# Preparing latent attention inside the last projection blocks, passing GLA and pool results through DRAM, and starting the projection in half blocks

## The chip, the cores and the metric

One core of a Trainium2 chip runs the whole kernel. The metric is the device time of one execution in microseconds, the median of several. The engines named below are TensorE (PE, with its weight loads as PEld), VectorE (DVE), ScalarE (ACT), GpSimd (POOL) and SyncE (SP), which issues most of the DMAs.

## The reference, cut to what matters

Two sequences (1024 and 512 tokens, so 1536 in all, width 1024) pass one encoder layer:

```python
h = rmsnorm(x, norm_g)
z = einsum('bsd,de->bse', h, w_in)          # c_q 256, c_kv 128, k_rope 64, gate_mla 512, u_pool 256, gate_pool 256,
                                            # q_gla, k_gla 128 each, v_gla 256, lr_fwd, lr_bwd 16 each, gate_gla 256
q  = rmsnorm(c_q) @ w_uq                    # 4 heads of 128 + 64 rotary
kv = rmsnorm(c_kv) @ w_ukv                  # 4 heads of 128 key + 128 value
p  = softmax((q_nope k_nope^T + rope(q_rope) rope(k_rope)^T) * MLA_SCALE)
o_mla = p v
o_pool = pool_mixer(u_pool)                 # centred means over windows 2, 4, 8, 16
o_gla = gla_mixer(...)                      # gated linear attention, forward and backward
mixed = concat(o_mla * silu(gate_mla), o_pool * silu(gate_pool), o_gla * silu(gate_gla))
y = rmsnorm(x + mixed @ w_out, final_norm_g)
```

## The kernel before

Features lie on the 128 partitions and tokens along the row, in three column blocks of 512 tokens (`BLK`, `TB = 3`). Every float32 product is made of three products of split operands (`product`, L75 to L79): each operand is a rounded `hi` and a remainder `lo`, and hi x hi, hi x lo and lo x hi are added in PSUM. ScalarE makes the `hi` parts; VectorE or GpSimd makes the `lo` parts by subtraction.

There are four phases, one after the other. Each ends only when all five engines have ended it, SP's waits on its DMAs among them.

- `phase_front` normalises x tile by tile (12 tiles of 128 tokens), turns the tiles with transposes into `h_hi` and `h_lo`, and multiplies by the input weights: 18 weight tiles (`ORDER`) times 3 column blocks are 54 blocks of 24 products (`project`). The first 6 blocks (`EARLY_BLOCKS`) are interleaved with the turns. Weight tile `o` is loaded by `load_w`, its hi part made by ScalarE in `split_hi`, its lo part by GpSimd in `split_lo`; one raw slot serves all tiles from the third on. Between the halves of the blocks stands the work of the gated linear attention (GLA) and the pooling (`mixing`, `compare`, `output`, `spread`), which ends around block 43. Tiles 7 to 14 of the order are the gates: `empty` copies them to `z_gate` and ScalarE's queue stores them to `gates_scratch`. The last three tiles are the latents `c_kv` and `c_q`, which stay in SBUF as rows of `z`, as do the results of the GLA; those of the pooling go to `pool_scratch` and come back.
- `phase_mla_prepare` normalises the latents, builds the query weights `w_q` (`w_uq` times `w_uk`), turns the tokens, makes the rotary queries (`rope_queries`, three column groups of 12 products) and rotates them on VectorE (L1317, L1322, L1289). SP stores them to `rope_scratch` in twelve DMAs (L1201) and then copies `mla_k_rope` onto the lower 64 partitions (L1204).
- `phase_mla_attend` makes scores, softmax and values for 4 heads.
- `phase_output` gates the mixed rows (GpSimd, `weight_gates`), splits them and multiplies by `w_out`, in a loop over pairs of token tiles, then adds x, normalises and stores.

The order of work on each engine is the order in which the code is written. Only semaphores join the engines, so a wait holds up all that follows in the same queue.

Of the kernel before, what the change touches and what calls it, by code (L numbers as in the profile page):

```python
# [44 lines left out]
def rows_of(t):  # L45
    return bass.ds(t * P, P)
# [28 lines left out]
def product(nc, out, a_hi, a_lo, b_hi, b_lo, first=True, last=True):  # L75
# [17 lines left out]
ORDER = (Z_LR, Z_U, Z_U + 1, Z_K, Z_V, Z_V + 1, Z_Q) + tuple(range(Z_FIRST_GATE, Z_FIRST_GATE + Z_GATES)) + \  # L93
    (Z_CKV + Z_GATES, Z_CQ + Z_GATES, Z_CQ + Z_GATES + 1)
FIRST_GATE_AT = 7
# [9 lines left out]

SPLITS = (32, 16, 8, 4, 2, 1)
# [16 lines left out]

def gla_point(i, half):

    return 2 * (i - FIRST_LEVEL_BLOCK) + half - 1


def phase_front(nc, cx, dram, gates_dram, pool_dram, k_rope_dram, h_hi, h_lo, z, psum, ident, sums):
# [5 lines left out]
    with ExitStack() as mem:  # L135
# [8 lines left out]
        sb("z_state_pad", [P, P // 4])  # L144
        gate_up = sb("z_gate_up", [P, 2, P])
# [42 lines left out]

        q, k = z[:, Z_Q, :], z[:, Z_K, :]
        values = z[:, Z_V:Z_V + 2, :]  # L190
# [5 lines left out]
        half_set = sem("n_half_set")  # L196
        squares_done = sem("n_squares_done")
# [25 lines left out]
        pool_back = sem("g_pool_back")  # L223
# [70 lines left out]
        def _(sp):  # L294
# [9 lines left out]

            load_x(0)
# [27 lines left out]
            sp.wait_ge(attn_mm, TILES)  # L333
            sp.dma_start(z[:, Z_U:Z_U + 2, :], pool_dram.rearrange("a p t -> p a t")).then_inc(pool_back, 16)
            sp.wait_ge(pool_back, 16)
# [4 lines left out]
        def _(act):  # L340
# [20 lines left out]
            def empty(i):  # L361
# [4 lines left out]
                if FIRST_GATE_AT <= o < FIRST_GATE_AT + Z_GATES:  # L366
                    if i >= TB * FIRST_GATE_AT + 2:
                        act.wait_ge(gate_stored[i % 2], 16 * ((i - TB * FIRST_GATE_AT) // 2))
                    nc.scalar.activation(stage[:, i % 2, :], bank, ACT.Copy).then_inc(z_emptied, 1)  # L369
                    if i > TB * FIRST_GATE_AT:  # L370
                        store_gate(i - 1)
                elif tile == Z_Q:
                    nc.scalar.activation(z[:, Z_Q, t], bank, ACT.Copy, scale=2.0 * GLA_Q_SCALE).then_inc(z_emptied, 1)
                else:
                    if tile == Z_V and tb == 0:
                        act.wait_ge(pool_step, POOL_STEPS)
                    if i == TB * (FIRST_GATE_AT + Z_GATES):
                        store_gate(i - 1)
                        act.wait_ge(o_mm, TILES)
# [1666 lines left out]
```

## Time and profile before

| | us |
|---|---|
| median of 3 runs | 852.72 |
| lowest to highest | 852.43 to 853.53 |
| the profiled execution | 853.92 |
| its span, first to last instruction | 852.1 |
| TensorE busy in the span | 767.0 (90%) |
| VectorE, ScalarE, GpSimd busy | 417.1, 333.3, 195.8 |
| mean granted TensorE clock | 0.966 |

All times in the rows are counted from the start of the span. Busy shares are means over phases with different limits, so they are read phase by phase: the front ends at 400.56 (TensorE's last product), the preparation at 457.96, attention at 695.58. TensorE has two clock levels, 2.4 and 1.2 GHz; the granted clock of a stretch is its mean share of the higher one. In the records from 0 to 30 us it reads 1.00 although the products stand 0.42 us apart, as they do elsewhere at 0.50; there the spacing is the better sign.

### The profile page before, as it was taken

The page shows a single profiled execution, that of the slowest core. Times are in us where ns is not written, and L with a number is a line of the kernel's source. Part 1 is how long each engine was busy: PE and PEld are TensorE (multiplying, and loading weights), DVE is VectorE, ACT ScalarE, POOL GpSimd, SP SyncE. Part 2 cuts the span into 40 slices and gives each one's busy share as a digit, 9 for nine tenths or more (in the row PEclk, how much of TensorE's full clock was granted, in tenths as well). Part 3 has the DMA queues.
Part 4 walks back from the last instruction along what each step waited for, and adds up shares of the span by engine and source line. Part 5 has one row for each costly group of instructions (what it writes and reads, how often), then busy time and mean ns, then how long its engine had stood idle before and what let it go on. Part 6 is the DMA issues. An engine that isn't in the chain of part 4 may idle for free. (4 is left out here: it accounts for less than half of the span.)

```text
span 852.1 us, 14303 instructions
## 1 busy us (share of the span) xinstructions
PE 767.0 (90%) x5936; PEld 637.4 (75%) x5936; DVE 417.1 (49%) x699; ACT 333.3 (39%) x570; POOL 195.8 (23%) x223
## 2 busy tenths in 40 slices
PE   3899999999999999998845899999999947999996
PEld 2786778788888878887744688888888845788885
DVE  5734766475565310000771566666667746433332
ACT  6441545334545323111530544444444553233321
POOL 2312125464454212110340000000000026233320
PEclk9999999999999999999676999999999987999999
DMA  7402021011111111400533000000033020444431
GB/s 274 126 12 63 26 95 41 27 40 64 64 50 40 54 65 60 148 23 22 167 100 88 12 13 14 13 20 18 13 106 131 1 98 27 147 149 148 148 123 49
DMA packets 32443, 61.37 MB, mean 72 GB/s; under 512 B 3296, under 2 KB 16000, under 8 KB 32384
## 3 DMA queue, kind: packets, MB, share of 16 engines
q1 hardware_dynamic: 26384, 46.36, 16.9%
q10 hardware_dynamic: 6000, 14.16, 4.3%
q8 instruction: 44, 0.72, 0.4%
q14 instruction: 15, 0.12, 0.0%
HBM read 42.42 MB, written 17.69 MB: 71 GB/s over the span
## 5 line engine op out<-in xcount | busy, mean ns | idle before, releaser
L77 PE MATMUL psum<-h_hi,z_w_hi 128*128 128x512 f32 x432 | 174.4, 404 | 3.8 <-DVE h_lo L697 3.8
L79 PE MATMUL psum<-h_hi,z_w_lo 128*128 128x512 f32 x432 | 169.0, 391 | 0.0
L78 PE MATMUL psum<-h_lo,z_w_hi 128*128 128x512 f32 x432 | 168.8, 391 | 0.0
L77 PEld LDWEIGHTS psum<-h_hi,z_w_hi 128*128 128x128 f32 x432 | 81.5, 189 | 24.3 <-DVE h_lo L697 4.6
L79 PEld LDWEIGHTS psum<-h_hi,z_w_lo 128*128 128x128 f32 x432 | 81.4, 189 | 17.6
L78 PEld LDWEIGHTS psum<-h_lo,z_w_hi 128*128 128x128 f32 x432 | 81.6, 189 | 16.4 <-issue 0.7
L1544 ACT ACTIVATE a_weights<-psum,a_bias,mla_q_scale 128x1024 f32<-128x1024 f32 (+1 forms) x48 | 51.1, 1064 | 103.8 <-DVE a_bias L1583 103.8
L77 PE MATMUL psum<-o_w_hi,o_m_hi 128*128 128x512 f32 x192 | 76.7, 400 | 15.4 <-DVE o_w_lo L1871 14.4
L78 PE MATMUL psum<-o_w_lo,o_m_hi 128*128 128x512 f32 x192 | 75.8, 395 | 0.0
L79 PE MATMUL psum<-o_w_hi,o_m_lo 128*128 128x512 f32 x192 | 75.7, 394 | 0.0
L1607 DVE TENSOR_TENSOR a_turned_lo<-psum,a_turned_hi 128x512 fp32r<-128x512 f32 x80 | 52.3, 687 | 41.7 <-ACT a_turned_hi L1561 41.7
L1752 POOL TENSOR_TENSOR mla_mixed<-mla_mixed,o_gate_first 128x512 f32 (+1 forms) x6 | 7.7, 1283 | 278.8 <-ACT o_gate_first L1787 278.8
L589 POOL TENSOR_TENSOR z_w_lo<-z_w_raw,z_w_hi 128x1024 fp32r<-128x1024 f32 x17 | 42.7, 2514 | 89.3 <-ACT z_w_hi L359 89.3
L828 DVE COPY_PREDICATED g_attn<-g_level_mask,psum 128x256 f32<-128x256 int32 x72 | 32.5, 451 | 59.0 <-ACT g_attn L476 56.9
L77 PEld LDWEIGHTS psum<-o_w_hi,o_m_hi 128*128 128x128 f32 x192 | 36.8, 192 | 24.9 <-issue 12.4
L1580 DVE TENSOR_REDUCE a_top<-psum 128x1 f32<-128x1024 f32 (+1 forms) x48 | 49.9, 1039 | 9.3 <-PE psum L1637 9.3
L381 ACT ACTIVATE z<-psum 128x512 f32<-128x512 f32 x27 | 15.9, 599 | 87.8 <-PE psum L79 87.8
L369 ACT ACTIVATE z_gate<-psum 128x512 f32<-128x512 f32 x24 | 14.3, 598 | 90.9 <-PE psum L79 90.9
L1645 PE MATMUL psum<-ident,a_weights 128*128 128x128 f32 x320 | 44.5, 276 | 5.5 <-DVE a_turned_lo L1607 5.5
L1645 PEld LDWEIGHTS psum<-ident,a_weights 128*128 128x128 f32 x320 | 35.7, 140 | 13.3 <-issue 8.9
L77 PE MATMUL psum<-a_turned_hi,mla_tokens_hi 128*128 128x256 f32 x160 | 44.8, 280 | 0.3 <-DVE a_turned_lo L1607 0.3
L79 PE MATMUL psum<-a_turned_hi,mla_tokens_lo 128*128 128x256 f32 x160 | 44.7, 279 | 0.0
(212 smaller groups left out, 1493.2 us busy)
## 6 DMA issues: line engine op xcount, KB each, us to landing
z_w_raw<-in_w_z_dram SPq DMA_DIRECT2D x17, 512.0 KB, 3.4
n_x_in<-in_x_dram SPq DMA_DIRECT2D x12, 512.0 KB, 4.1
gates_scratch<-z_gate ACTq DMA_DIRECT2D x24, 256.0 KB, 2.0
o_x_in<-in_x_dram SPq DMA_DIRECT2D x12, 512.0 KB, 3.5
out_dram<-o_y ACTq DMA_DIRECT2D x12, 512.0 KB, 2.6
o_w_raw<-in_w_out_dram SPq DMA_DIRECT2D x8, 512.0 KB, 9.6
a_q_rope<-rope_scratch SPq DMA_DIRECT2D x12, 256.0 KB, 2.6
o_gate_first<-gates_scratch SPq DMA_DIRECT2D x6, 512.0 KB, 5.3
```

The source lines that it names most:

```text
L77: nc.tensor.matmul(out, a_hi, b_hi, start=first, stop=False)
L78: nc.tensor.matmul(out, a_hi, b_lo, start=False, stop=False)
L79: return nc.tensor.matmul(out, a_lo, b_hi, start=False, stop=last)
L369: nc.scalar.activation(stage[:, i % 2, :], bank, ACT.Copy).then_inc(z_emptied, 1)
L381: nc.scalar.activation(z[:, place, t], bank, ACT.Copy).then_inc(z_emptied, 1)
L589: nc.gpsimd.tensor_tensor(w_lo[:, o % 2, :], raw_of(o)[:, :], w_hi[:, o % 2, :].bitcast(F32), ALU.subtract).then_inc(w_lo_ready, 1)
L828: nc.vector.copy_predicated(attn[:, t % 2, :, :], level_mask[:, n, :].bitcast(mybir.dt.int32).unsqueeze(1).broadcast_to([P, HEADS, CHUNK]) ...
L1544: nc.scalar.activation(weights[:, m % SLOTS, 0:count * P].rearrange("p (a k) -> p a k", k=BLK), psum[:, banks, :], ACT.Exp, bias=bias[:, m ...
L1580: nc.vector.tensor_reduce(top[:, m:m + 1], psum[:, banks, :], mybir.AxisListType.XY, ALU.max)\
L1607: nc.vector.tensor_tensor(turned_lo[at], psum[:, 4 + item % 2, :].rearrange("p (k q) -> p k q", k=4), turned_hi[at].bitcast(F32), ALU.subt ...
L1645: mm = nc.tensor.transpose(psum[:, 4 + item % 2, k * P:(k + 1) * P], weights[:, m % SLOTS, (4 * n + k) * P:(4 * n + k + 1) * P], ident[:, :])
L1752: nc.gpsimd.tensor_tensor(mla_mixed[:, :, rows_of(n)], mla_mixed[:, :, rows_of(n)], gate[s][:, 0:4, :], ALU.mult).then_inc(gated, 1)
```

## The change

1. `phase_mla_prepare` is gone; its steps stand inside `phase_front`. The latents move up in `ORDER`, ahead of the last two gate tiles: tile 13 is `c_kv`, 14 and 15 are `c_q`, 16 and 17 are gates. `prepare_attention` puts the steps between the half blocks of blocks 40 to 52. The latents are read from PSUM twice (a copy or scaled copy, and a Square for the sums of squares), and the lo part of `c_q` is made from PSUM.
2. The GLA and pool results are stored to `mix_scratch` and loaded per token tile in the output phase (`load_mix`).
3. The six early blocks are made in halves of 256 columns (`project_early`), the first after two tiles of x. The first two weights are loaded and split earlier.
4. TensorE first makes 14 products of zeros, and 5 after each of the first two turns (`keep_running`).
5. Tiles in SBUF are placed anew. `sum_latent_squares` sums four columns of 128 tokens a block, on a PSUM bank of its own.

TensorE, first instructions of the front. Before (L885 turns a tile of x, L77 to L79 are the products):

```order
L885 MATMUL psum<-ident,n_x_norm 128x128 x32
L77 MATMUL psum<-h_hi,z_w_hi 128x512
L78 MATMUL psum<-h_lo,z_w_hi 128x512
L79 MATMUL psum<-h_hi,z_w_lo 128x512
L77 MATMUL psum<-h_hi,z_w_hi 128x512
```

The same place now (L1479 are the products of zeros, L1195 turns a tile):

```order
L1479 MATMUL psum<-z_idle 128x512 x14
L1195 MATMUL psum<-ident,n_x_norm 128x128 x8
L1479 MATMUL psum<-z_idle 128x512 x5
L1195 MATMUL psum<-ident,n_x_norm 128x128 x8
L1479 MATMUL psum<-z_idle 128x512 x5
L1195 MATMUL psum<-ident,n_x_norm 128x128 x8
L77 MATMUL psum<-h_hi,z_w_hi 128x256
L78 MATMUL psum<-h_lo,z_w_hi 128x256
L79 MATMUL psum<-h_hi,z_w_lo 128x256
```

The first product now follows three turns, not four, and has half the columns.

SP, the end of the front and the preparation before (`rope_scratch` takes the turned queries; four such stores stand for each of three groups, the last group is shown):

```order
L1201 DMA rope_scratch<-p_rope0hi 4x32x512 [waits p_rope_hi]
L1201 DMA rope_scratch<-p_rope1hi 4x32x512 [waits p_rope_hi]
L1201 DMA rope_scratch<-p_rope0lo 4x32x512 [waits p_rope_lo]
L1201 DMA rope_scratch<-p_rope1lo 4x32x512 [waits p_rope_lo]
L1204 DMA mla_k_rope<-mla_k_rope 64x1536 [waits p_k_rope_hi]
L1117 UNCONDITIONAL_BRANCH [waits p_k_stacked,p_rope_stored]
```

SP at the end of the front now, from the load of the last weight tile on (the first of three groups is shown, then the end of the phase, after eight more stores):

```order
L386 DMA z_w_raw<-in_w_z_dram 128x1024 [waits z_w_lo_ready]
L446 DMA p_w_rope<-in_w_rope_dram 128x512 [waits z_w_lo_ready]
L448 DMA mla_k_rope<-mla_k_rope 64x1536 [waits p_k_rope_hi]
L453 DMA rope_scratch<-p_rope_split_147 4x32x512 [waits p_rope_hi]
L453 DMA rope_scratch<-p_rope_split_149 4x32x512 [waits p_rope_hi]
L453 DMA rope_scratch<-p_rope_split_146 4x32x512 [waits p_rope_lo]
L453 DMA rope_scratch<-p_rope_split_148 4x32x512 [waits p_rope_lo]
...
L152 UNCONDITIONAL_BRANCH [waits z_gate_stored0,p_rope_stored,z_gate_stored1,p_k_stacked,g_mix_stored]
```

The copy of `mla_k_rope` has moved ahead of the stores; their shape is unchanged, and the phase still ends with a wait for them.

The diff, cut to its core:

```diff
+ROPE_AT = {(51, 0): 0, (52, 0): 1, (52, 1): 2}
 # SP, front
+            load_w(0)
             load_x(2)
+            load_w(1)
             load_x(3)
-            load_w(0)
-            load_w(1)
...
+                if o == 12:
+                    store_mix(0)
...
+            sp.wait_ge(w_lo_ready, Z_TILES)
+            sp.dma_start(w_rope[:, :, :, :], dram["w_rope"]).then_inc(w_rope_loaded, 16)
+            sp.wait_ge(k_rope_hi, 1)
+            sp.dma_start(keep.k_rope[ROPE:P, :].bitcast(F32), keep.k_rope[0:ROPE, :].bitcast(F32)).then_inc(k_stacked, 16)
+            for tb in range(TB):
+                t = slice(tb * BLK, (tb + 1) * BLK)
+                for n, (part, ready) in enumerate(((1, rope_hi), (3, rope_hi), (0, rope_lo), (2, rope_lo))):
+                    sp.wait_ge(ready, 2 * tb + n % 2 + 1)
+                    sp.dma_start(rope_dram[:, n * HALF_ROPE:(n + 1) * HALF_ROPE, t],
+                                 rope_split[tb][part][:, :].bitcast(F32)).then_inc(rope_stored, 16)
+            sp.wait_ge(rope_stored, 64 * TB)
 # ScalarE, front
-                if n in (1, 2):
-                    split_hi(n - 1)
+                if n < 2:
+                    split_hi(n)
+                if i == 40:
+                    take_w_v()
+                if i == 41:
+                    take_w_q()
+                if i == 43:
+                    take_kv_mean()
+                if i == 44:
+                    fill_kv_rows()
+                if i == 46:
+                    take_ckv()
+                if i == 48:
+                    take_k_rope()
+                if i == 49:
+                    take_q_mean()
+                    take_tokens()
+                if i == 50:
+                    take_w_rope()
+                if i >= 51:
+                    take_rope(i - 51)
 # GpSimd, front
-                if n in (4, 5):
-                    split_lo(n - 4)
+                if n in (2, 3):
+                    split_lo(n - 2)
...
+            split_lo(17)
+            pool.wait_ge(k_rope_hi, 1)
+            subtract(keep.k_rope_lo[0:ROPE, :], k_swapped[:, :], keep.k_rope[0:ROPE, :]).then_inc(k_rope_lo, 1)
+            invert_means(rstd, q_mean_ready, q_root_step)
...
+            subtract(w_rope_lo[:, :, :, :], w_rope[:, :, :, :], w_rope_hi[:, :, :, :]).then_inc(w_rope_lo_ready, 1)
 # VectorE, front, after the GLA
+            split_tokens()
+            rotate(0)
+            split_rope(0)
+            rotate(1)
+            rotate(2)
+            split_rope(1)
+            split_rope(2)
 # TensorE, front
+            def prepare_attention(i, half):
+                if (i, half) == (W_Q_BLOCK, 0):
+                    make_w_q()
+                if half and SQUARES_AT < i <= SQUARES_AT + SQUARES:
+                    sum_latent_squares(i - 1 - SQUARES_AT)
+                if (i, half) == (KV_ROWS_BLOCK, 0):
+                    pe.wait_ge(kv_rows_ready, 1)
+                    pe.wait_ge(mixed, TB)
+                    turn_to_bank(kv_rows).then_inc(kv_rows_mm, 1)
+                if (i, half) == (TOKENS_BLOCK, 1):
+                    pe.wait_ge(ckv_ready, 1)
+                    turn_to_bank(ckv).then_inc(tokens_mm, 1)
+                if (i, half) in ROPE_AT:
+                    rope_queries(ROPE_AT[i, half])
+            def project_early(j):
+                o, tb, part = j % 2, j // 4, j // 2 % 2
+                pe.wait_ge(w_lo_ready, o + 1)
+                pe.wait_ge(lo_ready, 8 * tb + 4 * part + 4)
...
+            keep_running(14)
+            for n in range(3):
                 turn(n)
+                if n < 2:
+                    keep_running(5)
+            for j in range(2 * EARLY):
+                project_early(j)
+                if j + 3 < TILES:
+                    turn(j + 3)
 # output phase, SP and GpSimd
+                    sp.wait_ge(m_lo_ready, 2 * (2 * i + s) - 2)
+                    load_mix(i, s)
-                nc.gpsimd.tensor_tensor(z[:, Z_V:Z_V + 4, rows_of(n)], z[:, Z_V:Z_V + 4, rows_of(n)], gate[s][:, 4:8, :],
-                                        ALU.mult).then_inc(gated, 1)
+                pool.wait_ge(mix_loaded[s], 16 * i + 16)
+                nc.gpsimd.tensor_tensor(mix[s][:, :, :], mix[s][:, :, :], gate[s][:, 4:8, :], ALU.mult).then_inc(gated, 1)
```

`W_Q_BLOCK`, `KV_ROWS_BLOCK` and `TOKENS_BLOCK` are 41, 45 and 46; `SQUARES_AT` is block 39 and `SQUARES` 9.

## Rows read from the trace of the kernel before

**Rows 1.** Busy time by stretch: start:end, length, engines, clock, DMA share, GB/s.

```profile
67.03:400.56 333.53, 328.84 (x3569) 267.19 (x3568) 139.10 (x256) 122.58 (x211) 110.22 (x124) 1.00 0.15 54
400.56:457.96 57.40, 28.71 (x161) 26.45 (x161) 33.56 (x34) 19.55 (x21) 17.17 (x11) 0.68 0.43 126
```

**Rows 2.** Waits of TensorE from 400 us on: total us, times, longest.

```profile
PE psum L77 <- PEq L1117: 22.2, 1, 22.2
...
PE psum L77 <- DVE o_m_lo L1847: 1.0, 1, 1.0
```

**Rows 3.** SP's queue in order of time: start us, us, instruction.

```profile
419.82 0.66 SPq L1201 DMA_DIRECT2D rope_scratch<-p_rope0hi  x1
...
442.14 2.33 SPq L1201 DMA_DIRECT2D rope_scratch<-p_rope1lo  x1
444.51 0.90 SPq L1204 DMA_DIRECT2D mla_k_rope<-mla_k_rope  x1
458.22 1.28 SPq L1510 DMA_DIRECT2D a_q_rope<-rope_scratch  x3
```

**Rows 4.** Busy time by stretch in the preparation, columns as in rows 1.

```profile
421.00:424.00 3.00, 3.00 (x19) 3.00 (x19) 3.00 (x6) 0.03 (x1) 0.00 (x0) 0.60 0.24 43
...
426.00:436.00 10.00, 9.76 (x63) 9.06 (x61) 9.94 (x8) 3.03 (x3) 3.50 (x2) 0.83 0.26 102
...
446.00:452.00 6.00, 0.00 (x0) 0.00 (x0) 0.00 (x0) 0.00 (x0) 0.00 (x0) 0.50 0.93 146
```

**Rows 5.** TensorE at the start, and its first instruction after the early blocks.

```profile
8.04 1.97 PE L885 MATMUL psum<-ident,n_x_norm 128*128 128x128 f32 x8 [8.04 <-DMA ident<-in_ident_dram]
...
24.06 0.79 PE L77 MATMUL psum<-h_hi,z_w_hi 128*128 128x512 f32 x1 [3.60 <-DVE h_lo L697]
24.65 0.63 PE L78 MATMUL psum<-h_lo,z_w_hi 128*128 128x512 f32 x1
25.07 0.63 PE L79 MATMUL psum<-h_hi,z_w_lo 128*128 128x512 f32 x1
...
67.03 0.69 PE L913 MATMUL psum<-z,z_gate_up 32*128 32x512 f32 x1
```

**Rows 6.** TensorE's groups in the preparation: busy us, mean ns, idle before.

```profile
L1339 PE MATMUL psum<-p_ones,p_squares 128*128 128x1 f32 x72 | 9.4, 263 | 2.5 <-ACT p_squares L1241 2.5
L77 PE MATMUL psum<-mla_cq_hi,p_w_rope_hi 128*128 128x512 f32 x12 | 5.7, 471 | 4.0 <-DVE mla_cq_lo L1281 4.0
...
L1373 PE MATMUL psum<-p_w_uk_t,p_w_uq_t 128*128 128x128 f32 x16 | 2.8, 345 | 0.0
L1378 PE MATMUL psum<-ident,p_big 128*128 128x128 f32 x12 | 2.4, 382 | 0.0
```

**Rows 7.** TensorE, VectorE and GpSimd in the preparation, in order of time.

```profile
418.39 2.74 PE L1339 MATMUL psum<-p_ones,p_squares 128*128 128x1 f32 x24
...
416.07 0.68 DVE L1317 TENSOR_TENSOR p_turned<-psum,p_cos 128x512 f32<-128x512 f32 x1
...
433.25 3.15 DVE L1289 TENSOR_TENSOR p_rope0lo<-p_turned,p_rope0hi 128x512 fp32r<-128x512 f32 x1
...
432.42 3.44 POOL L1228 TENSOR_TENSOR mla_k_rope_lo<-p_k_swapped,mla_k_rope 64x1536 fp32r<-64x1536 f32 x1 [15.02 <-ACT mla_k_rope L1263]
```

**Rows 8.** ScalarE in the last blocks of the front: idle time in brackets.

```profile
389.71 0.60 ACT L381 ACTIVATE z<-psum 128x512 f32<-128x512 f32 x1 [4.84 <-PE psum L79]
395.15 0.60 ACT L381 ACTIVATE z<-psum 128x512 f32<-128x512 f32 x1 [4.84 <-PE psum L79]
```

**Rows 9.** VectorE's third and fifth normalisation, and GpSimd's first weight split.

```profile
12.60 1.29 DVE L689 SCALAR_TENSOR_TENSOR n_x_norm<-n_x_in,n_rstd,n_g_row 128x1024 f32<-128x1024 f32 x1 [0.21 <-POOL n_rstd L584]
...
19.44 3.36 DVE L689 SCALAR_TENSOR_TENSOR n_x_norm<-n_x_in,n_rstd,n_g_row 128x1024 f32<-128x1024 f32 x1 [0.47 <-POOL n_rstd L584]
...
19.37 2.35 POOL L589 TENSOR_TENSOR z_w_lo<-z_w_raw,z_w_hi 128x1024 fp32r<-128x1024 f32 x1
```

**Rows 10.** DMA issues of the output loop, 700 to 840 us: KB each, us to landing.

```profile
o_gate_first<-gates_scratch SPq DMA_DIRECT2D x5, 512.0 KB, 4.9
```

More of the change, by code:

```diff
@@ L144, in phase_front @@
         sb("z_state_pad", [P, P // 4])
+        assert sb.at == keep.consts_at
         gate_up = sb("z_gate_up", [P, 2, P])
@@ new lines, in rotate @@
+            def rotate(tb):
+                t, parts = slice(tb * BLK, (tb + 1) * BLK), rope_parts[tb]
+                one, two = psum[:, 2 + 2 * (tb % 2), :], psum[:, 3 + 2 * (tb % 2), :]
+                dve.wait_ge(rope_mm, tb + 1)
+                dve.wait_ge(z_done, rope_parts_free[tb])
+                for part, (half, table) in zip(parts, ((one, cos), (two, sin), (two, cos), (one, sin))):
+                    nc.vector.tensor_tensor(part[:, :], half, table[:, t], ALU.mult).then_inc(rope_step, 1)
+                for n, op in enumerate((ALU.subtract, ALU.add)):
+                    dve.wait_ge(rope_step, 4 * tb + 2 * n + 2)
+                    nc.vector.tensor_tensor(parts[2 * n][:, :], parts[2 * n][:, :], parts[2 * n + 1][:, :], op).then_inc(rope_turned, 1)
@@ new lines, in split_rope @@
+            def split_rope(tb):
+                parts, split = rope_parts[tb], rope_split[tb]
+                for n in range(2):
+                    dve.wait_ge(rope_hi, 2 * tb + n + 1)
+                    nc.vector.tensor_tensor(split[2 * n][:, :], parts[2 * n][:, :], split[2 * n + 1][:, :].bitcast(F32),
+                                            ALU.subtract).then_inc(rope_lo, 1)
+            split_w_q()
+            split_cq(0)
+            mix(TB - 1)
+            split_cq(1)
+            split_cq(2)
@@ new lines, in keep_running @@
+            def keep_running(count):
+                for _ in range(count):
+                    nc.tensor.matmul(psum[:, 5, :], idle[:, 0:P], idle[:, :], start=True, stop=True)
+            pe.wait_ge(idle_set, 1)
+            keep_running(14)
+            for n in range(3):
+                turn(n)
+                if n < 2:
[4 more added lines that the diff above has]
+                    turn(j + 3)
@@ L1383 @@
+STATE_AT = AFTER_Z + 2 * H_BYTES + D_MODEL * 4 + 4 * D_MODEL * 4 + 2 * BLK * 4
 class MlaKeep:
     def __init__(self, nc):
[L1387 to L1394 removed]
@@ L1415 @@
+        self.mix_first = rest("o_mix_first", [P, 4, P])
+        self.rest_at = rest.at
+        over_cq, over_w_q = Region(nc, cq_at), Region(nc, STATE_AT)
+        self.w_out = [(over_cq if k < 6 else over_w_q)(f"o_w_raw{k}", [P, D_MODEL]) for k in range(KT)]
 SEQ_TILES = tuple((t0 // P, n // P) for t0, n in SEQS)
```

701 lines of the change are left out of this document (362 added, 339 removed).

## The prediction

> **What bounds the kernel now.** I read the stretches of the span first, then TensorE's waits, then the timeline around the longest of them. In the long projection stretch TensorE is busy for 328.84 of 333.53 us [rows 1], so whatever is put there must either be hidden on the other engines or paid in TensorE time. The stretch after it is the loose one: of the 57.40 us from 400.56 to 457.96 TensorE is busy for 28.71, and the mean granted clock is 0.68 [rows 1]. One wait of 22.2 us ends it, released by the end of the phase and not by an engine [rows 2]. What is late there is in the queue of SP: twelve stores of the turned queries to `rope_scratch`, and one copy of `mla_k_rope` onto its lower half, issued at 444.51; the next phase starts at 457.96 [rows 3]. While the stores run the DMA share is 0.26 at 102 GB/s, that is some 4 of 16 engines, at all times [rows 4]. Twelve times 256 KB at 102 GB/s is 12 x 2.56 = 30.7 us. This stream, not the arithmetic, ends the preparation. At the start TensorE makes its first product at 24.06, and the sixth early block ends at 67.03 [rows 5]. The output phase is bound by TensorE: in its loop `o_m_lo` costs it 1.0 us in all [rows 2].
>
> **Part 1: the preparation moves into the front.** All 57.40 us go [rows 1]. TensorE gets back, among dense blocks:
> - 36 sums of squares, 72 records of 2.74 us for 24: 72 x 0.114 = 8.2 us [rows 6, 7];
> - 36 products for the rotary queries. A block of 24 takes 395.15 - 389.71 = 5.44 us, or 0.227 each [rows 8]: 8.2 us;
> - the query weights, 16 records, 2.8 us, and two turns of 12 transposes, 2.4 us each [rows 6]. These ran at a low clock. At most 7.6 us, at least half, 3.8; I take 4.4, nearer the lower end, since full-clock work surrounds them now. The 24 products that spread the root become 12 transposes.
>
> Sum 20.8 us (20.2 to 24.0). The last block therefore ends at 400.56 + 20.8 = 421.4, before the gain of part 3.
>
> What hides the rest: in these blocks ScalarE was idle 4.84 us before each 0.60 us eviction [rows 8]. It gets one more read (a Square) for nine blocks and about a dozen copies of 0.2 to 1.5 us. GpSimd gets two roots of some 3.1 us, two wide subtractions of 3.44 us (one is in [rows 7]) and two short ones. Both fit 15 blocks of 5.44 us. TensorE also waits on chains: the squares of block 39 to 41, the root, the spread at block 45, the transposes at 46, then split weights for the rotary products at 51. Followed in the order of each queue, the tightest is the last: GpSimd must do `k_rope_lo`, a root and `w_rope_lo` after its last weight split, which leaves me 2 to 3 us. I book no stall; if one of these covers is gone, TensorE stands in the block for the missing part, 2 to 10 us.
>
> **Part 2: the stores still end the phase.** Their shape is unchanged, 4x32x512, in the same queue, so I let them run as in the row: 2.56 us each. Call the end of the last block E. Counting back, block 53 takes 5.44, half a block 2.72, rotary group three 2.72, half a block 2.72, group two 2.72, block 51 5.44; so group one is done at E - 21.8. Before, the first store was issued 3.75 us after VectorE's first rotary product (416.07 to 419.82) [rows 3, 7], so now at E - 17.8. Full flow began some 2.8 us after that issue (43 GB/s in 421 to 424, 102 after) [rows 4]. From E - 15.0 the twelve need 30.7 us, without a hole: the second group's parts are ready by E - 9 and E - 3, while the first four stores keep the engines to E - 4.8. End at E + 15.7. Three or four gate stores of 256 KB, from ScalarE's queue, put 16 KB each on the same four engines, at 102/4 = 25 GB/s 0.6 us: about 2 us more. A landing and the step between the phases add 0.5 to 1. Attention starts at E + 18 (15 without the gate stores, 21 if each costs double). The copy of `mla_k_rope`, which kept the engines at a share of 0.93 from 446 to 452 [rows 4] behind the stores, is issued before them and leaves the path. So what was a wait of 22.2 us becomes one of 18 us, after which TensorE is as cold as before: no difference there.
>
> **Part 3: the start.** Before, four tiles of x had to be normalised and turned before product one. With half blocks of 256 columns two tiles do, and half the columns cost half the time. The first split weight comes earlier: its load stands ahead of the third tile of x, ScalarE splits it after tile 0 and GpSimd after root 2 (it was after tile 1 and root 4). But GpSimd's split now runs beside VectorE's third normalisation. Such a pass from SBUF takes 1.29 us alone and 3.36 beside that split [rows 9]; `p_rope0lo` took 3.15 beside a wide subtraction [rows 7]. So the third normalisation ends at about 16.0 instead of 13.9, the low half of tile 1 at 17.3, and the first product starts at 17.8, not 24.06. From there to 67.03 the old order needed 43.0 us: 32.6 for six blocks, 8 turns at some 0.85, and about 2.4 lost while products came every 0.42 us instead of 0.23 (24.65 to 25.07) [rows 5]. The new one needs 32.6 + 9 x 0.85 = 40.3 and ends at 58.1. That is 8.9 us early; for the last half blocks, which leave less time to split weight 2, I take off 0.9: 8.0 us (5.5 to 10). The zero products fill time in which TensorE waited for the first tile (to 8.04) [rows 5]; they cost nothing there. In the second gap 5 of them at 0.42 end 0.2 us late at worst.
>
> Whether they keep the clock up is the open part. Before, TensorE did turns with gaps between 8.04 and 24.06 and then found products at the lower pace [rows 5]. The Trainium skill (TensorE: Matmul & The Clock Gate, Part 4: PE-mode transpose) says that transposes do not count as work for the clock as products do; by that the last turns would undo the zero products. The trace agrees as far as it goes.
>
> **Part 4: results through DRAM.** Three stores of 512 KB run under the projection, where the DMA share is 0.15 [rows 1]; one load of 1.5 MB goes. In the output loop each tile loads 256 KB more, in rows of 512 bytes like the gates, whose 512 KB land 4.9 us after issue [rows 10]: 2.5 us more by proportion. TensorE takes 48 x 0.227 = 10.9 us a tile and waited 1.0 us in all [rows 2], and the second half of the gating needs the new tile only after the first. Zero; 0 to +3 us for the phase.
>
> **Sum.** 57.4 - 20.8 - 18 + 8.0 = 26.6 us less. The profiled execution took 853.9 us (span 852.1 and 1.8 around it), 1.2 above the median of the three runs: 853.9 - 26.6 = 827.3. I say 827.
>
> **Rivals.**
> - *A wait inside blocks 40 to 53*: one of the chains of part 1 is late, or GpSimd's and VectorE's passes slow each other as above. 3 to 10 us: 830 to 837. For: fifteen steps pass between four in-order queues. Against: ScalarE idles 4.84 of 5.44 us there [rows 8].
> - *The clock is low at the first product*, by the transpose rule. The lower pace costs 2.4 us, as before, and the weaker start perhaps 1 more: 830. The row on the pace bears it out; the ten zero products between the turns speak against.
> - *The stores do not bind*: the wait is some 4 us, for the last group's passes alone. 14 us less: 813. It needs the stores to use more than 4 engines; the unchanged shape speaks against.
> - *Slower than before: thin products lower the clock.* After 24 sums of squares in a row (one column each, 418.39 to 421) the granted clock in 421 to 424 was 0.60 [rows 4, 7]. Nine groups of them stand in blocks 40 to 48 now. A block at the lower level costs 5.44 us more; from five such blocks on the gain of 26.6 us is gone, and nine give 876. Against: each group is only 0.9 us long between half blocks of full products, and the projection stretch, which has such groups of two columns, reads a clock of 1.00 [rows 1].
> - *The change does nothing to the end*: every microsecond taken from the preparation comes back in the stores. Only if they started no earlier against E; they start 17.8 us before it. No chance of its own.
>
> **How the numbers follow.** Forecast (821 to 830) 0.58; wait inside the blocks 0.18; clock low at the start 0.12; stores not binding 0.07; low clock in the blocks 0.02; other losses of several sizes 0.03, a third of it slower than before. The range leaves out the stores that don't bind below 818 and the worst of the waits above 839. A measurement of this kernel tells 0.2% apart from no change. Faster 0.96, same 0.01, slower 0.03.
>
> **What would show it.** First product at about 18 us and the sixth early block's end at about 58; blocks of 5.44 us and no wait over 1 us in blocks 40 to 53; group one of the rotary products 22 us before the last block's end; a DMA share of about 0.26 at 100 GB/s for 30 us, and one wait of 15 to 21 us before attention; the first attention products every 0.42 us; the output phase 156 to 160 us long. The prediction is wrong if the stores spread over more engines, if blocks in 40 to 53 last over 7 us without an insert, or if the output loop waits for the mixed tile.

## The result, and the profile after

| | before | after |
|---|---|---|
| median, us | 853.12 (4 runs, 852.43 to 853.59) | 847.76 (4 runs, 846.21 to 848.11) |
| span of the profiled execution, us | 852.1 | 846.0 |

The ratio is 0.9937, 95% interval 0.9925 to 0.9950: 5.4 us faster where 26.6 were forecast, and outside the range. The sign was right. The span splits at four points, so that every term of the sum can be laid beside its measurement:

| stretch | before | forecast | after |
|---|---|---|---|
| start to the first product of `make_gates` | 67.0 | 59.0 | 67.5 |
| from there to the last product ahead of attention's wait | 333.5 (and 57.4 of preparation) | 354.3 | 361.8 |
| the wait ahead of attention | in the 57.4 | 18 | 23.4 |
| attention and output | 394.1 | 394.1 | 393.2 |
| sum | 852.1 | 825.4 | 846.0 |

The last three in the busy times by stretch of the kernel after (start:end, length, then busy us and instructions of PE, PEld, DVE, ACT and POOL, granted clock, DMA share, GB/s). They answer to [rows 1]:

```profile
67.50:429.35 361.85, 352.95 (x3717) 288.28 (x3716) 173.23 (x294) 138.78 (x235) 126.28 (x135) 0.99 0.19 64
429.35:452.79 23.44, 0.00 (x0) 0.03 (x1) 0.00 (x0) 0.60 (x1) 0.00 (x0) 0.60 0.28 103
452.79:846.00 393.21, 358.96 (x1968) 302.99 (x1968) 210.09 (x373) 158.54 (x281) 50.25 (x53) 0.97 0.24 77
```

The preparation is gone as a stretch. In its place stand 23.44 us in which no arithmetic engine works except ScalarE for 0.60, and the DMA share is 0.28. TensorE's waits in the kernel after (total us, times, longest) name three places:

```profile
PE psum L77 <- PEq L152: 23.4, 1, 23.4
...
PE psum L1479 <- DMA ident<-in_ident_dram: 8.1, 1, 8.1
...
PE psum L1369 <- ACT z_gate L515: 4.9, 1, 4.9
...
PE psum L77 <- DVE o_m_lo L1985: 0.7, 1, 0.7
```

The first answers to the 22.2 us of [rows 2]: one long wait was exchanged for another of the same size. The last, 0.7 us where [rows 2] have 1.0, says that the results that pass through DRAM cost the output loop nothing more. The other two are the start and the middle of the blocks.

**The start.** TensorE's timeline in the kernel after (start us, us, instruction; idle time and releaser in brackets):

```profile
8.12 6.18 PE L1479 MATMUL psum<-z_idle 128*128 128x512 f32 x14 [8.12 <-DMA ident<-in_ident_dram]
14.14 1.03 PE L1195 MATMUL psum<-ident,n_x_norm 128*128 128x128 f32 x8
...
19.86 1.16 PE L1195 MATMUL psum<-ident,n_x_norm 128*128 128x128 f32 x8 [1.29 <-DVE h_lo L931]
21.39 0.39 PE L77 MATMUL psum<-h_hi,z_w_hi 128*128 128x256 f32 x1 [0.37 <-POOL z_w_lo L797]
```

Zero products need no matrix for turning, yet they waited for `ident`. The line `pe.wait_ge(ident_loaded, 16)` stands in TensorE's queue above `keep_running(14)`; it is an unchanged line, and the diff puts the zero products behind it. So they ran from 8.12 to 14.14 in the way of the first turn, and not in the idle time ahead of it. [Rows 5] name the same releaser for the first turn before the change, `8.04 <-DMA ident`.

**The middle of the blocks.** ScalarE's timeline in the kernel after, and SP's queue just ahead of it:

```profile
321.53 0.34 ACTq L525 DMA_DIRECT2D gates_scratch<-z_gate  x1
...
328.50 0.60 ACT L515 ACTIVATE z_gate<-psum 128x512 f32<-128x512 f32 x1 [5.93 <-DMA gates_scratch<-z_gate]
```

```profile
317.95 0.33 SPq L386 DMA_DIRECT2D z_w_raw<-in_w_z_dram  x1
318.32 0.43 SPq L391 DMA_DIRECT2D mix_scratch<-z  x1
318.87 0.40 SPq L436 DMA_DIRECT2D p_cos<-in_rope_cos_dram  x1
319.31 1.31 SPq L437 DMA_DIRECT2D p_sin<-in_rope_sin_dram  x1
```

The first Square of the latents (line 515), for the first block of `c_kv`, writes a half of `z_gate`, the tile from which the last gates are stored; it must wait until that store has landed. The store was issued at 321.53, behind four large transfers of SP, and ScalarE could go on 7 us later. Gate stores take 2.1 us in the median of this kernel.

**The wait ahead of attention.** SP's queue in the kernel after, and the busy times of TensorE by stretch (length, PE busy, clock, DMA share, GB/s):

```profile
411.40 29.51 SPq L453 DMA_DIRECT2D rope_scratch<-p_rope_split  x12
452.76 1.43 SPq L1636 DMA_DIRECT2D a_q_rope<-rope_scratch  x3
```

```profile
25.00:30.00 5.00, 3.69 (x22) 0.77 0.50 148
30.00:35.00 5.00, 5.00 (x40) 0.89 0.52 170
...
330.00:335.00 5.00, 5.00 (x15) 0.51 0.00 0
...
437.00:442.00 5.00, 0.00 (x0) 0.50 0.26 101
442.00:447.00 5.00, 0.00 (x0) 0.50 0.26 102
```

The first store is issued 17.95 us before the last product ends (429.35 - 411.40); 17.8 was forecast. The flow is the forecast one as well, a share of 0.26 at 101 and 102 GB/s [rows 4]. But from 411.40 it takes 41 us until attention may load. The upper lines are for later: the clock fell at 25 to 35 us and behind the wait at 329.

### The profile page after: what moved, and what is told of

The parts are those of the page before. It is cut to its first block and busy times, and to the rows that moved or that the text cites. A ratio compares the mean times of both kernels' runs of the same rounds, so it can differ in the third digit from the quotient of the medians.

```text
span 846.0 us, 14631 instructions
## 1 busy us (share of the span) xinstructions
PE 767.9 (91%) x6092; PEld 644.0 (76%) x6092; DVE 416.4 (49%) x704; ACT 330.1 (39%) x574; POOL 195.1 (23%) x222
## 5 line engine op out<-in xcount | busy, mean ns | idle before, releaser
L77 PE MATMUL psum<-h_hi,z_w_hi 128*128 128x512 f32 (+1 forms) x480 | 184.5, 384 | 0.4 <-POOL z_w_lo L797 0.4
L79 PE MATMUL psum<-h_hi,z_w_lo 128*128 128x512 f32 (+1 forms) x480 | 178.5, 372 | 0.0
L78 PE MATMUL psum<-h_lo,z_w_hi 128*128 128x512 f32 (+1 forms) x480 | 178.1, 371 | 0.0
L77 PEld LDWEIGHTS psum<-h_hi,z_w_hi 128*128 128x128 f32 x480 | 91.8, 191 | 18.6 <-issue 2.2
L79 PEld LDWEIGHTS psum<-h_hi,z_w_lo 128*128 128x128 f32 x480 | 91.5, 191 | 16.2 <-issue 0.4
L78 PEld LDWEIGHTS psum<-h_lo,z_w_hi 128*128 128x128 f32 x480 | 91.8, 191 | 14.7 <-issue 0.7
L77 PE MATMUL psum<-o_w_hi,o_m_hi 128*128 128x512 f32 x192 | 76.3, 398 | 13.9 <-DVE o_w_lo L2009 13.3
L79 PE MATMUL psum<-o_w_hi,o_m_lo 128*128 128x512 f32 x192 | 75.7, 394 | 0.0
L77 PEld LDWEIGHTS psum<-o_w_hi,o_m_hi 128*128 128x128 f32 x192 | 36.7, 191 | 23.6 <-issue 12.1
L77 PE MATMUL psum<-a_turned_hi,mla_tokens_hi 128*128 128x256 f32 x160 | 45.3, 283 | 0.3 <-DVE a_turned_lo L1735 0.3
L78 PE MATMUL psum<-a_turned_lo,mla_tokens_hi 128*128 128x256 f32 x160 | 45.3, 283 | 0.0
L79 PE MATMUL psum<-a_turned_hi,mla_tokens_lo 128*128 128x256 f32 x160 | 45.3, 283 | 0.0
```

The lines of the kernel that those rows point to most:

```text
L77: nc.tensor.matmul(out, a_hi, b_hi, start=first, stop=False)
L78: nc.tensor.matmul(out, a_hi, b_lo, start=False, stop=False)
L79: return nc.tensor.matmul(out, a_lo, b_hi, start=False, stop=last)
```

## The experiments

Four questions: is the start lost to the place of one wait, do the stores bind through their shape, what held up the gate store, and what do the zero products bring. Each set has its own runs of the kernel before: 852.50 us for the first four, 853.02 for the next four, 853.12 for the last two. All ratios are to those.

### 1. The wait for `ident` behind the zero products

```
-            pe.wait_ge(ident_loaded, 16)
             def project_early(j):
...
             keep_running(14)
+            pe.wait_ge(ident_loaded, 16)
```

> The changed kernel with one wait moved: TensorE waits for the identity matrix after the first 14 products of zeros, not before them. In the changed kernel the zeros start at 8.12 us and last to 14.14, and the first turn follows. Theory (the zeros stand on the path, since the wait for the identity is ahead of them in the queue): the zeros run from about 1.5 to 7.6, the first turn starts at 8.1, the first real product at about 17 instead of 21.4, the first instruction after the early blocks at 61 to 63 instead of 67.5: 4.5 to 7 us less than the changed kernel, 839 to 843. Rival (the normalisation of x on the other engines sets the start anyway, as it did before the change): under 1 us less, 847.

Measured: 841.83 us (841.60 to 843.29), ratio 0.9879 [0.9863, 0.9896]. TensorE's timeline in this run:

```profile
1.45 6.28 PE L1478 MATMUL psum<-z_idle 128*128 128x512 f32 x14 [1.45 <-DVE z_idle L1073]
8.00 1.09 PE L1195 MATMUL psum<-ident,n_x_norm 128*128 128x128 f32 x8 [0.27 <-DMA ident<-in_ident_dram]
...
16.49 0.39 PE L77 MATMUL psum<-h_hi,z_w_hi 128*128 128x256 f32 x1 [0.37 <-POOL z_w_lo L797]
16.71 0.28 PE L78 MATMUL psum<-h_lo,z_w_hi 128*128 128x256 f32 x1
16.83 0.28 PE L79 MATMUL psum<-h_hi,z_w_lo 128*128 128x256 f32 x1
```

The zeros now run from 1.45, the first turn stands at 8.00 as before, and the first product at 16.49 instead of 21.39. `make_gates` begins at 61.1 instead of 67.5. One line that moves by a few places is worth 6 us, as much as the whole change brought.

### 2. No zero products

```
-            keep_running(14)
...
-                if n < 2:
-                    keep_running(5)
```

> The changed kernel without any product of zeros. Theory (zeros on the path, 6.0 us, against a lower clock for the first products, some 2.4 us lost before the change): 3 to 5 us less than the changed kernel, 843 to 845, with the first products 0.21 us apart for 256 columns. Rival (the zeros pay for themselves): slower than the changed kernel by up to 3 us.

Measured: 841.89 us (840.16 to 843.55), ratio 0.9874 [0.9853, 0.9895]: the same as experiment 1. TensorE's timeline in this run shows the other pace:

```profile
16.71 0.56 PE L77 MATMUL psum<-h_hi,z_w_hi 128*128 128x256 f32 x1
17.07 0.42 PE L78 MATMUL psum<-h_lo,z_w_hi 128*128 128x256 f32 x1
...
21.27 0.28 PE L77 MATMUL psum<-h_hi,z_w_hi 128*128 128x256 f32 x1
21.39 0.28 PE L78 MATMUL psum<-h_lo,z_w_hi 128*128 128x256 f32 x1
```

Products come 0.21 us apart until 21.1 and 0.12 after that; with the zeros they come 0.12 apart at once. So with the zeros TensorE stays at its high level through the turns. That was worth nothing: in experiment 1 the products reach the next tile early and TensorE waits for it, and here the slower products fill that wait. `make_gates` begins at 61.2.

### 3. Wide stores in the kernel after

The scratch of the rotary queries is laid out so that a store writes 128 rows in a row and not 4 groups of 32. Attention then loads each head in four pieces of 32 rows.

```
-                    sp.dma_start(rope_dram[:, n * HALF_ROPE:(n + 1) * HALF_ROPE, t],
+                    sp.dma_start(rope_dram[n, :, t],
...
-                sp.dma_start(q_rope[:, t].bitcast(F32), rope_dram[h, :, t]).then_inc(rope_loaded[b], 16)
+                for n in range(4):
+                    sp.dma_start(q_rope[n * HALF_ROPE:(n + 1) * HALF_ROPE, t].bitcast(F32),
+                                 rope_dram[n, h * HALF_ROPE:(h + 1) * HALF_ROPE, t]).then_inc(rope_loaded[b], 16)
```

> The changed kernel with rope_scratch laid out so that each of the twelve stores of turned queries has 128 rows as its outermost dimension instead of 4 (the loads of the attention become four of 32 rows each). In the changed kernel the stores run from 411.4 to about 452 at a DMA share of 0.26, and TensorE waits 23.4 us. Theory (a store with outermost dimension 4 uses 4 of the 16 engines, and this stream ends the phase): share while storing well over 0.5, the wait 3 to 5 us, the clock stays high at the start of attention, 19 to 22 us less than the changed kernel, 825 to 829. Rival (writing to DRAM or the queue is what limits to 100 GB/s): no change, 847.

Measured: 828.96 us (825.28 to 830.37), ratio 0.9720 [0.9688, 0.9752]. TensorE's wait, SP's queue and one stretch of this run:

```profile
PE psum L77 <- PEq L152: 3.9, 1, 3.9
```

```profile
411.55 17.21 SPq L453 DMA_DIRECT2D rope_scratch<-p_rope_split  x12
```

```profile
428.00:430.00 2.00, 1.49 (x7) 1.00 1.02 382
```

The wait is 3.9 us instead of 23.4, and SP issues the twelve stores over 17.21 us and not 29.51. At the end of the blocks (the last product ends at 429.48) the DMA engines are all busy at 382 GB/s, where the old layout gave 0.26 and 102. The Trainium skill (DMA: Bandwidth & Descriptors, "Why a DMA increments its semaphore by 16 and not by 1") says that a copy is split over the largest number of engines, up to 16, that divides the slowest dimension of both its patterns; the old pattern began with 4 and the new one begins with 128. By that rule the stores ran on 4 engines before and on 16 now, and the trace agrees with both: 0.26 is 4.2 of 16, and 1.02 is all. One thing expected did not come: the clock did not stay high at the start of attention, it read 0.66 in the 5 us behind the wait.

### 4. Wide stores alone, in the kernel before

> The kernel before, with the same wide stores alone. Theory: its wait of 22.2 us before attention shrinks to the landing of the copy of mla_k_rope, which is issued last, after VectorE and GpSimd end at about 443: attention starts at 447 to 450 instead of 458: 8 to 11 us less than before, 842 to 845. So more of the wait goes in the changed kernel, where the copy is early, than here. Rival (the copy of mla_k_rope itself takes the 12.9 us that it shows): 1 to 3 us less, 850 to 852.

Measured: 839.76 us (839.60 to 841.08), ratio 0.9856 [0.9839, 0.9872]. Its wait and its issues (KB each, median us to landing):

```profile
PE psum L77 <- PEq L1117: 9.0, 1, 9.0
```

```profile
rope_scratch<-p_rope0hi SPq DMA_DIRECT2D x3, 256.0 KB, 2.0
...
mla_k_rope<-mla_k_rope SPq DMA_DIRECT2D x1, 384.0 KB, 4.0
```

The edit is that of experiment 3. 22.2 us [rows 2] became 9.0, and the last 4 of these are mostly the copy of `mla_k_rope` (issued at 439.73, 4.0 to landing; attention starts at 444.20), which the change issues earlier. Attention starts 3 us sooner than the 447 expected at best: the last store is issued at 439.25 and not at 442.14. A layout changed in three places takes 12.7 us off the kernel before, over twice what the whole change took off. With wide stores in both, the change itself is worth 839.76 - 828.96 = 10.8 us, twice what it showed.

### 5. The cosine and sine tables later

```
                 if o == 15:
                     store_mix(1)
...
-                    sp.dma_start(cos[:, :], dram["rope_cos"]).then_inc(tables_loaded, 16)
-                    sp.dma_start(sin[:, :], dram["rope_sin"]).then_inc(tables_loaded, 16)
                 if o == 16:
...
                     store_mix(2)
+                    sp.dma_start(cos[:, :], dram["rope_cos"]).then_inc(tables_loaded, 16)
+                    sp.dma_start(sin[:, :], dram["rope_sin"]).then_inc(tables_loaded, 16)
```

> The changed kernel with the loads of the cosine and sine tables issued behind the last piece of the pool results and not behind the second; nothing else. In its trace TensorE waits 4.9 us at the sums of squares for a square that ScalarE takes, and ScalarE waited 5.93 us for a gate store that was issued 2.6 us behind the two table loads. Theory: the store shares its engines with the tables; without them it lands in about the 2.1 us that gate stores take elsewhere, the wait falls from 4.9 to 0 to 1.5, and the time is 3.5 to 5 us shorter, 843 to 844. Rival: the store is held up by the pool result and the 4 KB weight loads around it; then the wait stays over 3.5 and the time within 1 us of 847.7.

Measured: 843.01 us (839.28 to 846.52), ratio 0.9893 [0.9865, 0.9922]. The time is the expected one, but the wait is only halved:

```profile
PE psum L1369 <- ACT z_gate L515: 2.4, 1, 2.4
```

The tables were half of the delay. The weight load and the piece of `mix_scratch` still stand ahead of the gate store; experiments 9 and 10 take the piece away. Of the 4.7 us in span, 2.5 are this wait and 1.5 the clock behind it (0.91 from 320 to 340 us, where the kernel after has 0.83). Another 2.5 are the start: `make_gates` began at 65.0 and not at 67.5, since in this execution the fourteen zeros took 5.26 us instead of 6.18, and the clock did not fall at 25 us. That is no effect of the edit, and it fits the wide spread of the six runs. Against these stands the wait ahead of attention: it was 25.0 us here and 23.7 and 24.6 in experiments 1 and 2, with the same stores as in the kernel after, where it was 23.4. The blocks show the effect of the edit best: 357.9 us and not 361.8.

### 6. Thin gate stores

The gate stores of the last two gate tiles carry 16 of 512 columns; the first six gate stores are issued twice instead, to the places left unwritten. So this kernel leaves out most of the last two gate tiles; what stands in their place is copies of the first two.

```
-                act.dma_start(gates_dram[GATE_PLACE[g // TB], :, t:t + BLK], stage[:, g % 2, :])\
+                n = 16 if g >= GATES_FIRST_RUN else BLK
+                act.dma_start(gates_dram[GATE_PLACE[g // TB], :, t:t + n], stage[:, g % 2, 0:n])\
```

> The changed kernel, but the gate stores of blocks 48 to 55 carry 16 columns of 512, and those of the first eight gate blocks are issued twice, so that every byte of the scratch is written (two gate tiles are wrong). In the stretch in which the twelve rotary stores land (411.4 to 452.2 in the changed kernel's trace) five gate stores of 256 KB land too. Theory, by shares: the twelve stores alone take 12 x 2.56 = 30.7 us and the 18th us before the end of the blocks is when they start, so without the gate bytes the stretch is 33 to 36 us, the wait ahead of attention falls from 23.4 to 16 to 19, and the time is 4.5 to 7 us shorter, 841 to 843. Rival: what the stores lost beyond 30.7 us is their own cost for one (3.4 us each when several are queued), then the wait stays at 22 to 24 and the time within 1.5 us of 847.7. The extra eight stores are issued by ScalarE in the front, where they may cost up to 1 us.

Measured: 840.45 us (839.73 to 843.66), ratio 0.9865 [0.9843, 0.9887]. The wait of this run, which answers to the 23.4 of the kernel after:

```profile
PE psum L77 <- PEq L152: 17.8, 1, 17.8
```

Without the bytes of the gates the wait is 17.8 us, 1.8 more than the 16 to which the forecast of 18 comes without its 2 us for them. The gate stores cost the rotary stores 5.6 us, or up to 7.2 if the waits of 23.7 to 25.0 us in experiments 1, 2 and 5 are taken for the 23.4. The expectation counted five of them; in ScalarE's queue of the kernel after four are issued in the stream, from 413.07 to 430.0 us, so it is at least 1.4 each and not 0.6. The rival, a higher cost of the rotary stores themselves, is out as the main cause, but the 1.8 us that are left may be that. (Where the expectation speaks of eight added stores, the edit adds six.)

### 7 and 8. The edits together, with and without zeros

Experiment 7 is 1, 3 and 5 together; experiment 8 is 2, 3 and 5.

> Three edits to the changed kernel together: the wait for the turning matrix behind the fourteen zero products, the rotary scratch laid out so that each store has 128 destination rows, and the table loads behind the last pool result. If they add up by what each gave alone (6.0 and 18.7 measured, 3.5 to 5 expected), the time is 818 to 820 and attention starts near 423. Rival: with a front that ends earlier, the stores or ScalarE become late elsewhere and part of it is given back: 821 to 826. A kernel for use, which leaves nothing out.

> As the run before it, but with all 24 zero products taken out and not moved. Theory: the zero products bring nothing where the first turns wait for tiles anyway, so the time is within 1.5 us of the run before it (as the two single edits, 841.8 and 841.9). Rival: zeros keep the clock at its high level through the first products, which showed 0.21 us apart without them and 0.12 with them; over some 40 half-block products ahead of the next wait that is up to 3.5 us, and this run is that much longer. A kernel for use, which leaves nothing of the reference out.

Measured: 819.30 us (818.63 to 821.04), ratio 0.9607 [0.9585, 0.9629], and 814.79 us (814.40 to 816.74), ratio 0.9564 [0.9541, 0.9588]. The edits add up. But the two differ by 4.5 us, where 1.5 was the most expected, and the sign is that of neither theory. `make_gates` begins at 61.1 us in both, so the start is not the cause. (The profiled execution of 7 is its slowest of four, 821.04 us.) ScalarE's timeline of experiment 7, then of 8:

```profile
315.60 0.34 ACTq L525 DMA_DIRECT2D gates_scratch<-z_gate  x1
...
320.05 0.60 ACT L515 ACTIVATE z_gate<-psum 128x512 f32<-128x512 f32 x1 [3.41 <-DMA gates_scratch<-z_gate]
```

```profile
315.34 0.34 ACTq L525 DMA_DIRECT2D gates_scratch<-z_gate  x1
...
317.87 0.60 ACT L515 ACTIVATE z_gate<-psum 128x512 f32<-128x512 f32 x1 [1.49 <-DMA gates_scratch<-z_gate]
```

The same store, behind the same transfers at the same place, lets ScalarE go on after 4.5 us in one execution and 2.5 in the other. TensorE waited 2.4 and 0.5 us for it. The busy times of TensorE from 320 to 340 us, of experiment 7 and then of 8, show what came of it:

```profile
320.00:340.00 20.00, 19.30 (x95) 0.83 0.00 0
```

```profile
320.00:340.00 20.00, 20.00 (x113) 1.00 0.03 3
```

Behind the wait of 2.4 us the clock fell for some 7 us (0.83 of 20 us is 3.4 us of work lost); behind the wait of 0.5 it did not.

### 9 and 10. One more transfer away from the gate store

Both kernels again, and `store_mix(1)` moved next to `store_mix(2)`:

```
                 if o == 15:
-                    store_mix(1)
...
                 if o == 16:
...
+                    store_mix(1)
                     store_mix(2)
```

> The kernel without zero products, with wide stores and late tables (814.8 us), and besides the second piece of the pool results (512 KB) stored just ahead of the third and no longer 3.2 us ahead of the gate store for which ScalarE waits. Theory: that gate store now lands in about 2.1 us, TensorE's wait at the sums of squares is 0 to 1, the clock stays at 1.00 through 320 to 340 us in every execution, and the time is 0 to 1.5 us shorter, 813.3 to 814.8. Rival: the piece collides with the third piece and the tables instead, and a later gate store or the turned rotary rows become late: 1 to 4 us longer. A kernel for use, which leaves nothing out.

> As the run before it, with the 24 zero products in and the wait for the turning matrix behind the fourteen (819.3 us before the pool piece was moved). Theory: what set the two apart by 4.5 us (819.3 and 814.8) was not the zero products but the gate store: 2.4 us of wait against 0.5, and 3.4 us at the low clock behind it. With the store gone from ahead of it, both waits are under 1 us and the two times agree within 1.5 us: 813 to 816. Rival: the zero products themselves cost, at the start or through a clock that falls later; then this run stays 3 to 5 us above the run before it. A kernel for use, which leaves nothing out.

Measured: 813.96 us (813.15 to 814.44), ratio 0.9536 [0.9519, 0.9554], without zeros, and 815.63 us (814.79 to 816.82), ratio 0.9560 [0.9541, 0.9579], with them. In both the wait at the sums of squares is gone from the list of waits and the clock is 1.00 from 320 to 340 us. So 2.8 of the 4.5 us between 7 and 8 went with the gate store. What is left, 1.7 us, is just over the 1.5 expected. It does not lie at the start or in the blocks: the last product ahead of attention ends at 415.8 without the zeros and at 415.7 with them. Nor does it lie in attention. The two part in the output phase, behind short waits for its first split weights (0.2, 1.7 and 1.3 us in experiment 9, 0.7, 1.7 and 1.3 in 10); TensorE's timeline of experiment 9, then of 10:

```profile
677.21 0.50 PE L77 MATMUL psum<-o_w_hi,o_m_hi 128*128 128x512 f32 x1 [1.26 <-DVE o_w_lo L2008]
```

```profile
677.16 0.79 PE L77 MATMUL psum<-o_w_hi,o_m_hi 128*128 128x512 f32 x1 [1.26 <-DVE o_w_lo L2011]
```

Seven products stand 0.42 us apart behind this one in experiment 10, and none in 9: from 675 to 681 us the clock reads 0.72 and 1.00, and 0.28 of 6 us is 1.7 us. So in these two executions the zeros cost nothing themselves; what differs is one fall of the clock, 660 us behind them. Whether it has to do with them no run here says. Experiment 9, the best of all, by stretch (columns as in the kernel after):

```profile
61.00:415.81 354.81, 350.17 (x3717) 286.23 (x3716) 173.34 (x294) 138.80 (x235) 126.29 (x135) 1.00 0.21 69
415.81:419.74 3.93, 0.00 (x1) 0.04 (x1) 0.00 (x0) 0.60 (x1) 0.00 (x0) 0.93 0.66 245
419.74:812.30 392.56, 357.48 (x1968) 301.70 (x1968) 210.18 (x373) 158.53 (x281) 50.20 (x53) 0.97 0.24 77
```

That is 39.2 us less than the kernel before, against 5.4 for the change as it was made; and it is 25.8 less than experiment 4, where the wide stores stand alone.

## Why the prediction was wrong, step by step

**What bounds the kernel: right.** The narrow stores were the stream that ended the preparation, and they end the blocks now. Experiments 3 and 4 show it by taking the shape away.

**Part 1, the work put into the blocks: right in size, wrong in "I book no stall".** 20.8 us were forecast. Experiment 9, in which nothing waits there, has 354.8 - 333.5 = 21.3. The kernel after has 28.3. The 7.0 between them are 4.9 us of wait and some 2 us of clock behind it (0.51 from 330 to 335 us). The rival of a wait inside the blocks named the right size, 3 to 10 us, and the wrong cause. It looked at the chains of the arithmetic, the root and the split weights, and none of them was late by more than 1.0 us: beside the wait told next, TensorE has no longer one in the blocks from 300 us on, in the kernel after or in experiment 9. The wait came from the `z_gate` buffer: the change lets the squares reuse it, so the Square inherits the landing of the last gate store. The prediction listed the added passes of ScalarE and not their waits for buffers, and it did not ask what SP issues just ahead of that store. Four transfers stand there, three of them put there by the change; the wait is 4.3 to 5.1 us in experiments 1, 2, 3 and 6, which leave them where they are, and 2.4, 2.4, 0.5, 0 and 0 in 5, 7, 8, 9 and 10, which move them.

**Part 2, the wait ahead of attention: the mechanism right, one price too low.** The first store's issue was forecast 17.8 us ahead of the end of the blocks and is 17.95. The flow is right. The gate stores were priced at 2 us, three or four of them at 0.6. Four it was, and experiment 6 gives 5.6 us for them. That is 3.6 of the 5.4 us missed; the other 1.8 are missing without them too, and no run divides these further. The text gave 21 us for "each costs double", and even that fell 2.4 short. (Its 15 "without the gate stores" does not follow from its terms: 15.7 and 0.5 to 1 are over 16.) Why a gate store costs 1.4 us of the stream, where its bytes on the four shared engines make 0.6, stays open; nothing here separates the two queues on one engine.

**Part 3, the start: the step that failed worst.** 8.0 us gained were forecast, and 0.5 was lost. "The zero products fill time in which TensorE waited for the first tile (to 8.04) [rows 5]; they cost nothing there" is the sentence: it priced them by where idle time is and not by where they stand in the queue, and the row that it cites says that TensorE waited there for `ident` and not for the tile. Experiment 1 gives back 6.4 us at this point, so 6.0 of the forecast 8.0 are there. The 8.9 us of early arithmetic were optimistic too. In experiment 1 the first product is at 16.49, better than the forecast 17.8, but the sixth block ends 44.6 us later and not 40.3. The 288 products of 256 columns take 0.12 us each and not half of 0.227 (2 us in all), and TensorE waits 1.8 for the fourth tile. Besides, the forecast's terms for the old order, 32.6, 6.8 and 2.4, add up to 41.8 and not to its 43.0, and it left these 1.2 us out of the new order. VectorE and GpSimd in experiment 1 show where the fourth tile was held up:

```profile
17.25 3.42 DVE L923 SCALAR_TENSOR_TENSOR n_x_norm<-n_x_in,n_rstd,n_g_row 128x1024 f32<-128x1024 f32 x1 [1.84 <-POOL n_rstd L792]
...
17.18 2.40 POOL L797 TENSOR_TENSOR z_w_lo<-z_w_raw_second,z_w_hi 128x1024 fp32r<-128x1024 f32 x1
```

The normalisation took 3.42 us beside GpSimd's second split, as the fifth had beside a split in [rows 9]. The forecast put this on the third tile and the first split. There it fell the other way: the third normalisation took 1.28 us, and the split beside it 3.42. The kernel after loses 1.5 more between 25 and 35 us, where the clock fell (0.77, 0.89).

**Part 4, results through DRAM: right.** Zero was forecast; attention and output are 0.9 us shorter, and `o_m_lo` costs 0.7 instead of 1.0 [rows 2].

**The sum.** From the forecast of 825.4 us of span: 8.5 for the start, 7.5 for the blocks, 5.4 for the stores, -0.9 for the rest: 845.9, and 846.0 was measured.

**The rivals.** *The stores do not bind* named 4 us of wait; with wide stores it is 3.9, a right figure for a kernel that the change did not make. *The clock is low at the first product* did not occur in the kernel after (products 0.12 us apart), and experiment 2, where it does occur, costs nothing by it. The Trainium skill (TensorE: Matmul & The Clock Gate, Part 4: PE-mode transpose) says that transposes do not count as work for the clock. Experiment 2 fits it: three turns of eight transposes ran at the low pace, 1.94 to 1.97 us each, and so did the products behind them. It does not show it alone, since TensorE also stood idle for 1.75 and 1.30 us between the turns. In experiment 1, with fourteen zero products ahead of the turns and five in each gap, the turns took 1.09 to 1.16 us and the products stood 0.12 us apart. *Thin products lower the clock* is refuted: experiment 9 has all nine groups of them and reads 1.00. *The change does nothing to the end* came nearer than its "no chance of its own": of 26.6 us of gain, 21 were given back, though not by the one cause it named.

## What to carry to other kernels

Work that is meant to fill idle time must be priced by its place in the queue: look at the wait just above it, in the lines that the diff doesn't mark. When a pass gets a buffer that a store is leaving, the landing of that store joins the critical path, with all that other queues put ahead of it. And before moving work off a phase that a narrow DMA ends, look at the DMA: here a layout changed in three places was worth more than the move, and with it the move is worth twice what it was without.

## What the runs showed of the hardware

- A short wait can cost more than its length. After a wait of 4.9 us TensorE's clock was at 0.51 in the stretch of 5 us behind it; after one of 2.4 us it still fell (0.83 and 0.91 from 320 to 340 us in experiments 7 and 5), after 0.5 it did not. After waits of 1.8 and 1.3 us it fell in one execution and not in another: at 27.6 us in the kernel after and not in experiment 5, at 677 in experiment 10 and not in 9.
- The fall can come later than the wait. Ahead of attention a wait of 3.9 us was followed at once by products at the low level in experiments 8 and 9, and by some at the high level in 3, 7 and 10. TensorE's timeline, experiment 10 and then 8:

```profile
419.65 0.47 PE L77 MATMUL psum<-mla_cq_hi,mla_w_q_hi 128*128 128x512 f32 x1 [3.95 <-PEq L152]
```

```profile
419.99 0.77 PE L77 MATMUL psum<-mla_cq_hi,mla_w_q_hi 128*128 128x512 f32 x1 [3.93 <-PEq L152]
```

  But in experiment 10 the products stood 0.42 us apart from 421.3 on, and over the first 5 us the clock read 0.66 there and 0.68 in 8. The first product behind a wait does not say what the wait costs.
- The same start can differ by 2.5 us between executions through the clock alone (`make_gates` at 67.5 in the kernel after, at 65.0 in experiment 5, with the same instructions up to there).
- A gate store of 256 KB lands in 2.1 us in the median of the kernel after. Behind four large transfers of SP's queue ScalarE was let go 7.0 us after it was issued; behind two of them 4.5 us after in experiment 7 and 2.5 in 8, with the same neighbours.
- A VectorE pass with both inputs in SBUF and a GpSimd pass slow each other, and either can be the one that pays: the normalisation took 1.28 us beside a split of 3.42, and 3.42 beside a split of 2.40 (experiment 1).
